# Memory keys and values token-major from whole weight rows, with the nine token tiles' first norms between the weight blocks

## The reference, cut to what matters

```python
def rmsnorm(x, g):
    y = x * lax.rsqrt(jnp.mean(x * x, axis=-1, keepdims=True) + EPS)
    return y * g

mk = (mem @ w_k)      # mem: 256 memory tokens x 1024, both weights 1024 x 1024
mv = (mem @ w_v)      # both are outputs, and the cross-attention reads them later
proj = rmsnorm(x, norm_mix) @ w_in      # first projection of all 1032 tokens
...                   # short convolution, gated linear attention, output projection
x = x + y             # then rmsnorm, cross-attention into mk and mv, rmsnorm, mixture of experts
y_out = rmsnorm(x, norm_final)
```

## Time and profile before

| what | value |
|---|---|
| median of three runs | 1266.28 us |
| the profiled execution's own time | 1268.61 us |
| span of its trace | 1266.9 us |
| mean granted TensorE clock | 0.944 of full |
| TensorE matmul busy | 1155.2 us, 91% |
| VectorE busy | 453.0 us, 36% |
| ScalarE busy | 370.4 us, 29% |

### The profile page before, as it was taken

The page is one execution under the profiler, slowest core; times in us unless marked ns, Lnnn a source line. Parts: engine busy times, 40 slices in busy tenths (PEclk is TensorE's granted clock), DMA queues, the critical chain, the costliest instruction groups (busy, mean ns, idle before and its releaser), DMA issues.

```text
span 1266.9 us, 14386 instructions
## 1 busy us (share of the span) xinstructions
PE 1155.2 (91%) x6014; PEld 873.4 (69%) x6014; DVE 453.0 (36%) x778; ACT 370.4 (29%) x568; POOL 106.0 (8%) x118
## 2 busy tenths in 40 slices
PE   4878989899999999899999988998999699999994
PEld 4876889898888879688699843436887554444441
DVE  3542350163543442632311076224314622323222
ACT  3551451121111103521111122224111124454542
POOL 1000000000000000000000000000000114444433
PEclk8998989999999998999999977999999599999998
DMA  7644101111101312432121333333421798888721
GB/s 188 184 120 150 34 28 40 34 34 34 34 18 37 86 50 66 150 117 81 39 64 37 150 133 132 113 136 120 162 100 69 288 399 303 352 318 319 298 92 49
DMA packets 100443, 163.29 MB, mean 129 GB/s; under 512 B 20354, under 2 KB 73874, under 8 KB 93972
## 3 DMA queue, kind: packets, MB, share of 16 engines
q1 hardware_dynamic: 85972, 136.91, 31.2%
q0 software_dynamic: 14400, 25.40, 5.8%
HBM read 140.84 MB, written 48.50 MB: 149 GB/s over the span
## 4 chain that ended last, share of the span: by engine, by line
PE 82%; DVE 7%; ACT 5%; issue 2%; SPq 1%; DMA 1%; POOL 0%; DVEq 0%; POOLq 0%; ACTq 0%
PE G L1204 16%; PE G L1160 11%; PE G L1162 10%; PE G L1161 10%; PE G L687 9%; PE G L709 4%; PE G L1497 2%; PE G L691 2%; PE G L1453 2%; PE T L1469 2%; PE T L679 2%; PE T L1383 1%; PE T L1219 1%; PE G L1469 1%; PE G L714 1%
## 5 line engine op out<-in xcount | busy, mean ns | idle before, releaser
L1160 PE MATMUL G<-act_hi,w_hi 128*128 128x344 f32 (+2 forms) x920 | 304.1, 331 | 22.7 <-DVE w_lo L1782 8.5
L1161 PE MATMUL G<-act_lo,w_hi 128*128 128x344 f32 (+2 forms) x920 | 295.8, 321 | 0.0
L1162 PE MATMUL G<-act_hi,w_lo 128*128 128x344 f32 (+2 forms) x920 | 295.3, 321 | 0.0
L1160 PEld LDWEIGHTS G<-act_hi,w_hi 128*128 128x128 f32 (+1 forms) x920 | 176.5, 192 | 37.2 <-issue 20.0
L1161 PEld LDWEIGHTS G<-act_lo,w_hi 128*128 128x128 f32 (+1 forms) x920 | 176.7, 192 | 3.2 <-issue 1.2
L1162 PEld LDWEIGHTS G<-act_hi,w_lo 128*128 128x128 f32 (+1 forms) x920 | 176.4, 192 | 2.0
L1204 PE MATMUL G<-wt,act_hi 128*128 128x512 f32 (+1 forms) x576 | 159.9, 400 | 9.3 <-DVE act_lo L2002 4.9
L1204 PEld LDWEIGHTS G<-wt,act_hi 128*128 128x128 f32 (+1 forms) x576 | 101.5, 178 | 41.1 <-issue 9.0
L1782 DVE TENSOR_TENSOR w_lo<-arena,w_hi 128x1024 fp32r<-128x1024 f32 (+1 forms) x49 | 58.8, 1202 | 177.4 <-ACT w_hi L1512 177.4
L687 PE MATMUL G<-wring,misc 128*128 128x512 f32 x256 | 115.0, 603 | 1.2 <-ACT misc L756 1.2
...
L1204 PE MATMUL G<-wt,act_lo 128*128 128x512 f32 (+1 forms) x288 | 90.6, 396 | 0.0
...
## 6 DMA issues: line engine op xcount, KB each, us to landing
...
arena<-in_w_in_dram SPq DMA_DIRECT2D x24, 512.0 KB, 3.9
arena<-in_x_prompt_dram SPq DMA_DIRECT2D x16, 512.0 KB
d_x<-arena SPq DMA_DIRECT2D x16, 512.0 KB
...
```

Source lines behind the costliest of these rows:

```text
L1160: pe.matmul(out, a_hi, b_hi, start=first, stop=False)
L1161: pe.matmul(out, a_hi, b_lo, start=False, stop=False)
L1162: return pe.matmul(out, a_lo, b_hi, start=False, stop=last)
```

## The change

- The weight blocks of keys and values are now 128 whole **rows** of `w_k` or `w_v` (4 KB pieces). The stationary operand is a 128x128 piece of the transposed memory tokens, held in buffers of its own (`mem_hi`, `mem_lo`), and 512 weight columns move: twelve matmuls for each block (`mem_block`). All eight blocks accumulate in PSUM, keys first, then values; nothing is copied out between blocks.
- The result is token-major, so "memout" with its 32 transposes goes. Keys are copied out after their last block (VectorE one tile, ScalarE the other), written out during the value blocks ("kout"), and transposed back for the spill in sixteen transposes between later blocks ("memT"). Values are copied out at the end ("vev"), partly while the last block runs.
- The memory tokens no longer use columns of `act_hi`, so all nine tiles are normed between the blocks, in natural order. The transposes ("fw0") are entries of their own, after the blocks given by `FWD_AFTER`; the norm stands two blocks earlier, or ahead of the first block. From the second token tile on they all use one PSUM buffer, and wait for the low half of the tile before.
- Mean and epsilon move into ScalarE's root as scale and bias, in every norm; VectorE's instructions at L1856 and L976 and their two semaphores go, and ScalarE waits for its own row sum.
- SP loads the two token tiles ahead of the convolution state; the memory tiles have a semaphore each; the PSUM groups of the later column blocks start with the other parity.

The core of the diff:

```diff
+    FWD_AFTER = (1, 3, 4, 5, 6, 9, 11, 13, 14)
+    KEYS_T = (10, 12)
+    assert len(FWD_AFTER) == TILES and len(KEYS_T) == MB
     for n in range(2 * KB):
+        if n == 0:
+            order += [("norm", t) for t in range(TILES) if FWD_AFTER[t] < 2]
         order.append(("block", n))
-        if n >= 2 and n % 2 == 0 and early:
-            order.append(early.pop(0))
-    order += early + [("memout", 0), ("norm", 0), ("norm", 1)]
-    order.append(("st", 0))
+        order += [("norm", t) for t in range(TILES) if FWD_AFTER[t] == n + 2]
+        order += [("fw0", t) for t in range(TILES) if FWD_AFTER[t] == n]
+        if n == KB - 1:
+            order.append(("kev", 0))
+        if n == KB:
+            order.append(("kev", 1))
+        if n == KB + 1:
+            order.append(("kout", 0))
+        order += [("memT", m) for m in range(MB) if KEYS_T[m] == n]
+    order += [("vev", 0), ("memout", 0), ("st", 0)]
     for n in range(2 * KB, at[("cc", 0)]):
...
         def fwd_at(f):
 
-            return fwd[f % 2] if f < MB + TILES else T[:, :, :]
+            return G[0][:, 1:3, :] if f == 1 else T[:, :, :]
 
...
                     act.wait_ge(s[f"y_out{st % 2}"], 32 * (st // 2))
                 act.activation(fin[st % 2], acc[st % 2], ACT.Square, accum_out=cst[:, st, 0:1]).then_inc(s["c_sq"], 1)
-                act.wait_ge(s["c_ms"], st + 1)
-                act.activation(cst[:, st, 2:3], cst[:, st, 1:2], ACT.Sqrt).then_inc(s["c_rt"], 1)
+                act.wait_ge(s["c_sq"], st + 1)
+                act.activation(cst[:, st, 2:3], cst[:, st, 0:1], ACT.Sqrt, scale=1.0 / D, bias=epsb[:, 0:1]).then_inc(s["c_rt"], 1)
 
...
                 if st == 0:
                     dve.wait_ge(s["fg_in"], 16)
-                dve.wait_ge(s["c_sq"], st + 1)
-                v.tensor_scalar(cst[:, st, 1:2], cst[:, st, 0:1], 1.0 / D, EPS, ALU.mult, ALU.add).then_inc(s["c_ms"], 1)
                 dve.wait_ge(s["c_rt"], st + 1)
...
                 if n >= RAW:
                     sp.wait_ge(s["split_done"], n - RAW + 1)
-                if by_rows[n]:
+                if by_rows[n] or mem_row[n]:
...
                         load_x(norm_seq[j + 2])
+                elif what == "kout":
+                    sp.wait_ge(s["mem_dve"], K_DVE)
+                    sp.wait_ge(s["mem_act"], K_ACT)
+                    for m in range(MB):
+                        sp.dma_start(new_mk[0, 0, m * P:(m + 1) * P].rearrange("m h d -> m (h d)"),
+                                     mtm[0][:, m, :]).then_inc(s["mem_out"], 16)
                 elif what == "memout":
-                    sp.wait_ge(s["mem_tm_ev"], 2 * MB)
-                    for o, (dst, r) in enumerate(((new_mk, mtm[0]), (new_mv, mtm[1]))):
-                        for m in range(MB):
-                            sp.dma_start(dst[0, 0, m * P:(m + 1) * P].rearrange("m h d -> m (h d)"),
-                                         r[:, m, :]).then_inc(s["mem_out"], 16)
+                    sp.wait_ge(s["mem_dve"], V_DVE)
+                    sp.wait_ge(s["mem_act"], KT_ACT + 1)
+                    sp.wait_ge(s["mem_act"], KT_ACT + 2)
+                    for m in range(MB):
+                        sp.dma_start(new_mv[0, 0, m * P:(m + 1) * P].rearrange("m h d -> m (h d)"),
+                                     mtm[1][:, m, :]).then_inc(s["mem_out"], 16)
+                    sp.wait_ge(s["mem_act"], KT_ACT)
                     sp.dma_start(d_mkT, region("vtm", MB * D, KB * MEM)).then_inc(s["mk_spill"], 16)
                 elif what == "us":
...
                     ins.then_inc(s["big_done"], 1)
+
+            def mem_block(n):
+
+                kind, k = kinds[n]
+                pe.wait_ge(s["split_done"], n + 1)
+                for m in range(MB):
+                    if kind == "memv" and k == 0 and m == 1:
+                        pe.wait_ge(s["mem_dve"], K_DVE)
+                    for c in range(2):
+                        w0 = slice(c * 4, (c + 1) * 4)
+                        ins = mm3(k_acc[m][:, c, :] if kind == "memk" else v_acc[m][c], mem_hi[m][:, k, :], mem_lo[m][:, k, :],
+                                  w_hi[:, n % 2, w0, :].rearrange("p a b -> p (a b)"), w_lo[:, n % 2, w0, :].rearrange("p a b -> p (a b)"),
+                                  k == 0, k == KB - 1)
+                    if kind == "memv" and k == KB - 1 and m == 0:
+                        ins.then_inc(s["mem_v0"], 1)
...
-                    pe.wait_ge(s["nlo_done"], f - 1)
+                    pe.wait_ge(s["nlo_done"], f)
                 for k in range(KB):
...
+                        pe.wait_ge(s["mem_act"], KT_ACT + 2)
+                    if mem_row[i]:
+                        mem_block(i)
+                    elif (kind, b) == ("mq", 0):
                         first_query_block()
...
-                elif what == "norm":
-                    j, stage, t = nseq[i], i // TILES, i % TILES
-                    if stage == 0:
-                        pe.wait_ge(s["h_done"], j + 1)
-                        forward(MB + j, hb[j % 2], rows[t])
+                elif what == "memT":
+                    pe.wait_ge(s["mem_dve"], K_DVE)
+                    pe.wait_ge(s["mem_act"], K_ACT)
+                    if i >= 1:
+                        pe.wait_ge(s["mem_act"], K_ACT + i)
+                    for k in range(KB):
+                        ins = pe.transpose(back[:, k // 4, (k % 4) * P:(k % 4 + 1) * P], mtm[0][:, i, k * P:(k + 1) * P], ident[:, :])
+                    ins.then_inc(s["mem_tr"], 1)
+                elif what == "fw0":
+                    j = nseq[i]
+                    pe.wait_ge(s["h_done"], j + 1)
+                    forward(MB + j, hb[j % 2], rows[i])
...
                 act.wait_ge(raw_in[n % RAW], 16 * (n // RAW + 1))
-                if nth[n] >= 2:
+                if mem_row[n]:
+                    if n >= 2:
+                        act.wait_ge(s["mem_mm"], n - 1)
+                    act.copy(w_hi[:, n % 2, :, :].rearrange("p a b -> p (a b)"), raw_rows(n)).then_inc(s["hi_done"], 1)
+                    return
+                if nth[n] < 2:
+                    act.wait_ge(s["mem_mm"], 2 * KB - 1 + nth[n])
+                else:
                     act.wait_ge(s["big_done"], use(by_cols[nth[n] - 2]) + 1)
...
-                for x in ahead:
-                    square(x)
-                    jx, rx = nseq[x], rows[x % TILES]
-                    act.wait_ge(s["ms_done"], jx + 1)
-                    act.activation(ssum[0:rx, jx, 2:3], ssum[0:rx, jx, 1:2], ACT.Sqrt).then_inc(s["rt_done"], 1)
-                if stage == 0:
-                    late(i)
-                else:
+                square(i)
+                act.wait_ge(s["sq_done"], j + 1)
+                act.activation(ssum[0:r, j, 2:3], ssum[0:r, j, 0:1], ACT.Sqrt, scale=1.0 / D,
+                               bias=epsb[0:r, 0:1]).then_inc(s["rt_done"], 1)
+                if stage:
                     if t >= 1:
                         late(i - 1)
...
+                        act.copy(mtm[0][:, 1, :].rearrange("p (a n) -> p a n", a=2), k_acc[1]).then_inc(s["mem_act"], 1)
+                elif what == "memT":
+                    act.wait_ge(s["mem_tr"], i + 1)
+                    act.copy(mkT_w[:, :, i * P:(i + 1) * P], back.rearrange("p a (k n) -> p (a k) n", n=P)).then_inc(s["mem_act"], 1)
+                elif what == "vev":
+                    act.wait_ge(s["mem_v0"], 1)
+                    act.copy(mtm[1][:, 0, 0:512], v_acc[0][0]).then_inc(s["mem_act"], 1)
+                    act.wait_ge(s["mem_mm"], 2 * KB)
+                    act.copy(mtm[1][:, 1, :].rearrange("p (a n) -> p a n", a=2), OUT[0]).then_inc(s["mem_act"], 1)
                 elif what == "split":
                     if by_rows[i]:
                         split_rows_hi(i)
...
 
-                def mean_square(x):
-                    jx, rx = nseq[x], rows[x % TILES]
-                    dve.wait_ge(s["sq_done"], jx + 1)
-                    v.tensor_scalar(ssum[0:rx, jx, 1:2], ssum[0:rx, jx, 0:1], 1.0 / D, EPS, ALU.mult, ALU.add).then_inc(s["ms_done"], 1)
...
-                    if stage == 0:
-                        mean_square(same[p + 1])
-                else:
+                if stage and p + 1 == len(same):
                     late(i)
 
             def bcast(ap, shape):
                 return ap.to_broadcast(shape)
 
...
+                    while behind:
+                        late(behind.pop(0))
                     if what != "begin":
                         read_out(i)
+                elif what == "fw0":
+                    behind.append(i)
+                elif what == "kev":
+                    if i == 0:
+                        dve.wait_ge(s["mem_mm"], KB)
+                        v.tensor_copy(mtm[0][:, 0, :].rearrange("p (a n) -> p a n", a=2), k_acc[0]).then_inc(s["mem_dve"], 1)
+                elif what == "vev":
+                    dve.wait_ge(s["mem_v0"], 1)
```

(1 more changed line is left out.)

98 lines of the change are left out of this document (48 added, 50 removed).

## The result

Four runs of the changed kernel gave a median of 1249.55 us (1246.13 to 1251.33), four of the kernel before, run beside them, 1265.89 (1264.97 to 1267.59). The profiled execution took 1250.03 with a span of 1248.1, against 1268.61 and 1266.9 before: 18.6 less where the prediction had 25.6. The kernel is faster, and the median lies inside the stated range of 1231 to 1251, near its upper end; the forecast proper, 1237 to 1244, was missed. By the medians 9.3 us of the promised 25.6 are missing in the first set and 4.4 in the second, by the first pair of profiles 7.0, and the rest of this text is about them.

What follows compares the result with a forecast made beforehand. TensorE held 82% of the span, with time lost in waits, half clock and removable work. Savings of 22.4 + 3.0 + 0.2 = 25.6 gave 1243.0 us profiled, 1240.7 against the median; forecast 1237 to 1244, range 1231 to 1251.

Steps and rivals of the forecast that it cites:

- "lr" 22.4 earlier: First stage: blocks, transposes, clock loss and 7.6 us of stalls sum to "lr" starting at 79.6 for 102.0.
- transposes that the prediction priced too high: First stage: twelve groups of transposes at 1.08 us each, 13.0 us in all.
- block 3's weights: First stage, SP's load: issued about 18.3, landing after 3.7, ready at 24.3, due at 25.4; cost nothing.
- The stalls of 2.5 behind blocks 4 and 5: Forwards there wait on one PSUM buffer: chain 5.3, of which a block covers 2.79; 2.5 us twice, 5.0.
- Rival 2, the clock: Handoff stalls drop TensorE's clock, 1.4 us lost after each, at most blocks 1 to 6; 1243.5 to 1262, chance 0.14.
- "lr" 3.0 shorter: Stage "lr" runs at full clock, 11.2 us for 14.20, its copy-out not waiting for the value outputs.
- the time from "lr" to the end: Behind the start of "lr": same distance to the end but for 3 us; growth would show the prediction wrong.
- Mean and epsilon, 0.2: Norms: a root with scale and bias reads no more elements; 0.2 us saved, on one later tile's chain.
- The page's rule: Weight loads: full rate from 512 bytes, so rows win nothing; block 3 ready 2.8 later, result 1242.4.
- Rival 1: First stage: loads bound it at 165 GB/s, "lr" starts at 84, 4.3 later; 1245 us, chance 0.13.
- Rival 3: First stage: handoffs serialize, 10.0 us per tile, "lr" starts at 108.5; about 1273 us, slower, chance 0.03.
- Rival 4: First stage: single PSUM buffer and early norms cost nothing, the 7.6 us go; 1233 us, chance 0.12.

Runs made afterwards that it cites:

- Run 2: Changed kernel with thirteen constant loads issued by GpSimd's queue instead of SP's: 1245.15 us, ratio 0.9815 to the kernel before.
- run 1: Changed kernel with FWD_AFTER = (2, 4, 5, 7, 8, 10, 11, 13, 14), spreading the forwards: 1239.76 us, ratio 0.9775.
- run 8: Changed kernel with memory key and value weights fetched as 128 columns (512-byte pieces) instead of rows: 1291.52 us, not comparable because routing differs.
- run 11: Changed kernel with extra 128x512 matmuls, result unread, filling TensorE's waits ahead of block 3 and two forwards: 1244.53 us, ratio 0.9808.
- run 10: Changed kernel with spread forwards, constants on GpSimd's queue, early table load and 16 added transposes ahead of block 0: 1237.04 us, ratio 0.9746.
- run 12: The kernel of run 10 with forwards moved to after blocks 3, 4, 6, 7, 9, 10, 12, 13, 14: 1238.44 us, ratio 0.9746.
- run 3: Changed kernel with sixteen unread 512-column matmuls filling TensorE's pause ahead of block k0: 1247.78 us, ratio 0.9823.
- run 4: Changed kernel with mean and epsilon back on VectorE in every norm: 1246.51 us, ratio 0.9826.
- run 5: Changed kernel unaltered, measured again as a second set of five runs: 1246.59 us, ratio 0.9831.
- run 6: Kernel before with only mean and epsilon moved into ScalarE's root, in all norms: 1272.14 us, ratio 1.0023.

## Why the prediction was right, and where it wasn't

**"lr" 22.4 earlier: 20.4 measured.** Step by step, with the times at which TensorE reached each point:

| point | forecast | measured | what it shows |
|---|---|---|---|
| block 0 | 12.9 | 12.41 | each memory tile now has its own wait, and the transposes started at 4.42 for 6.25; the table load, moved from 0.81 to 6.45, took 1.28 of it back |
| block 1 | 18.8 | 18.12 | stall 0.6 for 1.7; block 0 almost wholly at half clock, 2.3 lost for 1.4 |
| block 3 | 25.4 | 26.76 | a wait of 1.94 for a cost of nothing |
| forward of tile 1 | 28.2 | 31.22 | block 3 at half clock, 1.6 |
| forward of tile 2 | 34.6 | 37.76 | wait 2.73 for 2.5 |
| forward of tile 3 | 41.0 | 45.21 | wait 2.17 for 2.5, forward and block 5 behind a fallen clock |
| "lr" | 79.6 | 81.62 | 36.4 for 38.6: groups of transposes 0.79 to 0.88 each for 1.08, the 8-row tile 0.59 and the state 0.35 |

That the forecast came within 2.0 us is in part luck: four of these steps are 4.9 us late together, and 2.9 of it is made up by the others, most by transposes that the prediction priced too high.

The step that failed is block 3's weights. The prediction let its load leave when tile 0's product was done, 18.3, and priced the landing at 3.7; SP was still issuing constants until 19.1, and the landing took 4.8. The front part of the text itself says that SP issues some fourteen constants ahead of the list. By forecast the weights were ready at 24.3 and due at 25.4; in fact they were ready at 26.7 and due at 24.8, since the blocks ahead came sooner. Of the 2.4 us by which they were late, 1.3 are the issue and 1.1 the landing. Run 2 takes the constants away and the wait with them.

**The stalls of 2.5 behind blocks 4 and 5.** Right: 2.73 and 2.17, and run 1 shows that it is the crowding of forwards that makes them. The prediction's own chain, 5.3 behind transposes of 1.08, makes 6.4 from one forward to the next; at full clock it took 6.57 (runs 8 and 11).

**Rival 2, the clock.** It came true in part: two spells, not from block 1 to 6. Its short price, 1.4 for each, was 1.6 behind block 3 (a place that it doesn't name) and 0.2 to 0.9 behind the forward. That TensorE's idling comes ahead of the spells is shown best by block 0: in the kernel before and in every changed profile without the added transposes it began at half clock, and in runs 10 and 12, with them, at full clock. That a later pause drops the clock is not certain each time: in run 8 two waits of 2.71 and 2.74 passed at 1.00, and the waits ahead of block 3 in runs 3, 4, 5 and 12 (1.54 to 1.88) passed at full spacing where those of 1.94 (first profile, block 3) and 1.90 (run 10, block 2) did not. The Trainium skill, page "TensorE: Matmul & The Clock Gate", Part 1, says that activity releases the throttle; runs 10 and 11 agree, where added work on TensorE alone took block 0 from spacings of 0.43 to 0.23 and kept the clock at 1.00 from 18 to 50 us.

**"lr" 3.0 shorter: 2.8 measured,** and no wait of its copy-out for the outputs. But the prediction also says that the time from "lr" to the end shrinks by 3 and by no other amount, and names its growth as a sign of being wrong. In the profiled execution it grew by 1.6; in run 5 it shrank by 4.4. The 2.8 and a further 1.6 of the first profile went to k0 (1.3, run 3), to the long form of the recurrence (2.9, run 5) and small change. In the eleven profiles of the changed kernel and its kin the time behind "lr"'s start is 1160.3 to 1166.7, before 1164.9: a gain of 3 in a stretch of this length lies inside what differs from profile to profile, and one profiled execution can't show it.

**Mean and epsilon, 0.2:** nothing to be seen (run 4), and in the kernel before a loss of 0.2% (run 6). The sentence that a root with scale and bias reads no more elements is true and misleading: it takes 0.29 for 0.20.

**The page's rule** moved the forecast by 1.7, to 1242.4. The measured landings of the new rows (5.4, 4.8) lie between the two prices that the prediction set against each other, 3.7 and 6.5, so neither was the right one to take. The rows also gain time on SP, which the prediction doesn't price: 1.40 for the first three loads' issue, 4.26 before.

**Rivals 1, 3 and 4.** Apart from block 3 the loads did not bound the stage: 184 GB/s, and no wait for a weight behind that block. The handoffs did not run one behind another: behind the fourth forward only block 8 waited. Rival 4 comes closest to what run 1 reached: with another order alone "lr" started at 74.6, 5.0 earlier than forecast.
